# Input projection of a two-layer hybrid trunk: values projected last, pooling products inside the projection's last tiles

## The reference, cut to what matters

```
h      = rms_norm(x) * (1 + scale) + shift
proj   = h @ w_in                      # 1024 -> 1280 columns
q,k,v,u = split(proj, [512, 640, 768]) # 8 query heads, 2 key/value heads of 64; u: 4 groups of 128
q,k    = rms_norm per head; rotary positions on latent tokens; cached context keys and values joined
attn   = softmax(q k^T / 8) v          # in blocks of 128 queries
pooled = window mean(u) - u            # windows 2, 4, 8, 16, one per group
mixed  = pooled @ w_pool[group] * pool_scale
x      = x + gate * (concat(attn, mixed) @ w_out)
x      = x + gate * (silu(a) * g) @ w_down   # a, g: conv over rms_norm(x) @ w_up
```

## Time and profile before

| what | us |
|---|---|
| median of 3 runs | 1485.87 (1483.33 to 1486.97) |
| profiled execution, its own time | 1485.4 |
| its span | 1483.6 |
| TensorE busy | 1436.1 (97%) |
| VectorE busy | 896.4 (60%) |
| ScalarE busy | 518.3 (35%) |
| GpSimd busy | 388.3 (26%) |

### The profile page before, as it was taken

One profiled execution on the slowest core, in us unless ns is written; L12 is line 12 of the kernel. 1 busy time (PEld: TensorE's weight loads), 2 busy tenths in 40 slices (PEclk: granted clock), 3 DMA queues, 4 the chain that ended last, 5 costly groups with the idle time before them and its releaser, 6 DMA issues.

```text
span 1483.6 us, 25242 instructions
## 1 busy us (share of the span) xinstructions
PE 1436.1 (97%) x10077; PEld 1382.2 (93%) x10077; DVE 896.4 (60%) x1372; ACT 518.3 (35%) x743; POOL 388.3 (26%) x259
## 2 busy tenths in 40 slices
PE   6998899999999999999999989999999999999996
PEld 4888689999999999999999868999999999999996
DVE  3637867898875578784865788249844323444423
ACT  3325772442331123222242577234223112322321
POOL 0145001134431023443214600213433101333310
PEclk9999999999999999999999999999999999999998
DMA  9642004344444334334413200123322222222321
GB/s 340 211 172 74 1 2 129 99 128 129 141 143 127 127 105 150 124 113 138 138 40 86 61 2 1 54 90 103 114 80 82 79 68 72 71 71 80 89 59 71
DMA packets 190718, 147.05 MB, mean 99 GB/s; under 512 B 4256, under 2 KB 178984, under 8 KB 188584
## 3 DMA queue, kind: packets, MB, share of 16 engines
q1 hardware_dynamic: 189440, 145.32, 31.3%
q10 hardware_dynamic: 1192, 0.52, 0.1%
HBM read 142.94 MB, written 2.88 MB: 98 GB/s over the span
## 4 chain that ended last, share of the span: by engine, by line
PE 89%; DVE 5%; issue 2%; ACT 2%; DMA 1%; POOL 0%; SPq 0%; DVEq 0%; ACTq 0%; POOLq 0%
PE pair L1175 71%; PE pair L1192 5%; PE pair L1440 3%; PE pair L1476 3%; PE pair L1453 2%; DVE mod_acc L860 1%; PE pair L1262 1%; DVE w_lo L837 1%; DVE q_st L1006 1%; DMA xin<-in_x_sample_dram 1%; PE pair L1293 1%; PE pair L1245 1%; DVE conv L1119 0%; DVE x L932 0%; DMA mod_acc<-in_w_mod_dram 0%
## 5 line engine op out<-in xcount | busy, mean ns | idle before, releaser
L1175 PE MATMUL pair<-in_hi,w_hi 128*128 128x320 f32 x1792 | 410.5, 310 | 3.3 <-DVE w_lo L837 3.3
L1175 PE MATMUL pair<-in_hi,w_lo 128*128 128x320 f32 x1792 | 408.3, 309 | 0.0
L1175 PE MATMUL pair<-in_lo,w_hi 128*128 128x320 f32 x1792 | 408.3, 309 | 0.0
L1175 PEld LDWEIGHTS pair<-in_hi,w_hi 128*128 128x128 f32 x1792 | 298.9, 188 | 8.9 <-issue 4.3
L1175 PEld LDWEIGHTS pair<-in_hi,w_lo 128*128 128x128 f32 x1792 | 299.6, 188 | 0.0
L1175 PEld LDWEIGHTS pair<-in_lo,w_hi 128*128 128x128 f32 x1792 | 299.5, 188 | 0.0
L1119 DVE SCALAR_TENSOR_TENSOR conv<-pair,vec,conv 128x127 f32<-128x127 f32 x352 | 168.7, 541 | 200.1 <-ACT conv L775 199.9
L529 POOL TENSOR_TENSOR silu_a<-silu_a,conv 128x640 f32<-128x640 f32 x44 | 110.9, 2520 | 562.8 <-DVE conv L1119 562.8
L837 DVE TENSOR_TENSOR w_lo<-w_raw,w_hi 128x1024 fp32r<-128x1024 f32 (+1 forms) x152 | 201.7, 1327 | 62.4 <-ACT w_hi L550 62.1
L550 ACT ACTIVATE w_hi<-w_raw 128x1024 fp32r<-128x1024 f32 (+1 forms) x88 | 103.3, 1174 | 353.9 <-PE pair L1175 322.7
L775 ACT ACTIVATE conv<-pair,vec 128x640 f32<-128x640 f32 x88 | 77.8, 886 | 413.7 <-PE pair L1175 405.8
(11 more groups left out here) (171 smaller groups left out, 1544.9 us busy)
## 6 DMA issues: line engine op xcount, KB each, us to landing
w_raw<-in_w_up_dram SPq DMA_DIRECT2D x88, 512.0 KB, 3.9
mod_raw<-in_w_mod_dram SPq DMA_DIRECT2D x64, 512.0 KB, 4.4
w_raw<-in_w_down_dram SPq DMA_DIRECT2D x32, 704.0 KB, 4.6
w_raw<-in_w_in_dram SPq DMA_DIRECT2D x20, 512.0 KB, 4.0
w_first<-in_w_mod_dram SPq DMA_DIRECT2D x8, 1024.0 KB, 13.8
w_raw<-in_w_out_dram SPq DMA_DIRECT2D x16, 512.0 KB, 4.2
mod_raw<-in_w_mod_dram SPq DMA_DIRECT2D x4, 1024.0 KB, 6.7
mod_acc<-in_w_mod_dram SPq DMA_DIRECT2D x4, 1024.0 KB, 6.4
```

The lines of the kernel that those rows point to most:

```text
L1175: ins = pe.matmul(dst[:, a:a + HALF_T], w[:, s, k, :], rhs[:, kk, a:a + HALF_T], start=first and r == 0, stop=last and r == 2)
```

## The change

Ten tiles stay ten tiles, but the values come last: n = 5 to 8 are the queries and n = 9 the values.

- Key factors are made as columns like those of the queries (`rk`, 10 columns), inside the tile behind the keys, at k = 2. ScalarE's root and VectorE's reciprocal work on 10 columns. At k = 6 ten products of 64 result partitions with the identity (`k_factors`) spread them to a 128 x 640 PSUM area, which VectorE's scaling of the keys reads.
- The pooling product of a group (`mix_product`, two products instead of three) stands at k = 2 of tiles 6, 7, 8 and 9, the statistics of a query tile at k = 5. ScalarE copies a mixed group, scaled, to `u` (`mix_copy`). GpSimd parts the four groups into `in_hi` and `in_lo`, after its rotary work and after the projection's end.
- `keep_busy(15)` is gone.
- The values are transposed behind `scores(1)` and copied by ScalarE behind exponential 0.
- `q_hi(3)`, `q_low(3)` stand in unit 1, `q_hi(NQ)`, `q_low(NQ)` in unit 3 (they stood ahead of attention and in unit 2). The parting of the second output tile's weights (`hi` and `lo` of tile N_IN + 1) moves from the projection's last tile to unit 4. The two output transfers of new keys and values are issued in unit 6.
- The exponential's table is loaded by a `preload_act_table` ahead of attention. `k_low` is parted in two, one head group each, so scores of the first four heads wait for the first only.

```diff
-    IN_U, IN_K, IN_V, IN_Q = 0, NPOOL, NPOOL + 1, NPOOL + 2
-    IN_COLUMN = [AW + 2 * KV + P * g for g in range(NPOOL)] + [AW, AW + KV] + [P * t for t in range(NQ)]
+
+    IN_U, IN_K, IN_Q, IN_V = 0, NPOOL, NPOOL + 1, NPOOL + 1 + NQ
+    IN_COLUMN = [AW + 2 * KV + P * g for g in range(NPOOL)] + [AW] + [P * t for t in range(NQ)] + [AW + KV]
...
+                pool.wait_ge(s_lin, tile_in(L) + N_IN)
+                for g in range(NPOOL):
+                    pool.wait_ge(s_pc, L * NPOOL + g + 1)
+                    pool.tensor_copy(in_hi[:, NQ + g, :], u[:, g, 0:T]).then_inc(s_phi, 1)
+                    pool.wait_ge(s_phi, L * NPOOL + g + 1)
+                    pool.tensor_tensor(in_lo[:, NQ + g, :], u[:, g, 0:T], in_hi[:, NQ + g, :].bitcast(F32),
+                                       ALU.subtract).then_inc(s_plo, 1)
...
+                def mix_copy(g):
+
+                    act_e.wait_ge(s_pm, L * NPOOL + g + 1)
+                    act_e.activation(u[:, g, 0:TP], mix_p, ACT.Copy, scale=v(L, V_PS, g))
+                    act_e.activation(u[:, g, TP:T], mix_s, ACT.Copy, scale=v(L, V_PS, g)).then_inc(s_pc, 1)
...
+                    if n == IN_K:
+                        act_e.wait_ge(s_pkt, L + 1)
+                        act_e.activation(keys[:, TP:TP + PAST], pair[2][:, T:T + P], ACT.Copy).then_inc(s_pk, 1)
                         k_std()
...
+                        act_e.preload_act_table(ACT.Exp)
...
-                        if i == 2:
+                        if i == 3:
                             q_hi(NQ)
...
+                    if i == 0:
+                        values()
+                    if i == 1:
+                        q_hi(3)
+                    if i == 4:
+                        hi(tile_in(L) + N_IN + 1, (N_IN + 1) % 2, NK)
+                    if i == 6:
+                        new_cache_out()
...
+                    if i == 1:
+                        q_low(3)
+                    if i == 3:
                         q_low(NQ)
+                    if i == 4:
+                        lo(tile_in(L) + N_IN + 1, (N_IN + 1) % 2, NK)
...
-                    for hf in range(2):
-                        a = hf * HALF_T
-                        ins = pe.matmul(lin[2][:, a:a + HALF_T], head_ones, sq[:, E % 2, a:a + HALF_T], start=True, stop=True)
+                    for b in range(NT):
+                        c = K_STAT + 2 * b
+                        ins = pe.matmul(pair[3][:, c:c + 2], sq[:, E % 2, b * P:(b + 1) * P], head_ones[:, 0:P:HD],
+                                        start=True, stop=True)
                 else:
...
+            def k_factors(L):
+
+                pe.wait_ge(s_krs, L + 1)
+                pe.wait_ge(s_pk, L + 1)
+                for b in range(NT):
+                    for g in range(2):
+                        ins = pe.matmul(k_spread[g * HALF:(g + 1) * HALF, b * P:(b + 1) * P],
+                                        rk[:, 2 * b + g:2 * b + g + 1].to_broadcast([P, HALF]), ident, start=True, stop=True)
+                ins.then_inc(s_ksp, 1)
+
+            def mix_product(L, g):
+                if g == 0:
+                    pe.wait_ge(s_wp, 16 * (L + 1))
+                    pe.wait_ge(s_kn, L + 1)
+                else:
+                    pe.wait_ge(s_pc, L * NPOOL + g)
+                pe.wait_ge(s_pooled, L * NPOOL + g + 1)
+                pe.matmul(mix_p, wp[:, g, :], u[:, g, U_P:U_P + TP], start=True, stop=True)
+                pe.matmul(mix_s, wp[:, g, :], u[:, g, U_S:U_S + TS], start=True, stop=True).then_inc(s_pm, 1)
...
+                    def between(k, n=n):
+
+                        if n == IN_K + 1 and k == 2 or n > IN_K + 1 and k == 5:
+                            q_stat(L * NE + e_of(n - 1))
+                        if n == IN_K + 1 and k == 6:
+                            k_factors(L)
+                        if n > IN_Q and k == 2:
+                            mix_product(L, n - IN_Q - 1)
+                    linear(tile_in(L) + n, n % 2, NK, in_hi, in_lo, wait_k=between)
...
-                keep_busy(15)
-                for g in range(NPOOL):
-                    pe.wait_ge(s_pooled, L * NPOOL + g + 1)
-                    if g < 2:
...
+                def transpose_values():
+                    pe.wait_ge(s_free, L * (N_IN - NPOOL) + IN_V - IN_K + 1)
+                    pe.wait_ge(s_kout, L + 1)
+                    pe.wait_ge(s_pc, (L + 1) * NPOOL)
+                    for b in range(NT):
+                        ins = pe.transpose(pair[2][:, b * P:(b + 1) * P], v_feat[:, b * P:(b + 1) * P], ident)
+                    ins.then_inc(s_vt, 1)
...
                 scores(1)
+                transpose_values()
```

More of the change, by code:

```diff
@@ L220, in build @@
         MODP = 832
+        mix_s, mix_p = pair[2][:, 0:TS], pair[3][:, P:P + TP]
+        k_spread = pair[2][:, 0:T]
+        K_STAT = NQ * NT * 2
         V_BMOD, V_CONVB, V_N1, V_N2, V_PS, V_QG, V_KG = (0, 0), (0, 48), (0, 92), (0, 100), (0, 108), (0, 112), (0, 113)
@@ L1033, in _ @@
                         dve.tensor_copy(u[:, n, U_S:U_S + TS], src[:, TP:T]).then_inc(s_u, 1)
-                    lo(N + 2, n % 2, NK)
-                    if e_of(n - 1) is not None:
-                        if e_of(n - 1) == 0:
-                            k_norm()
-                        shuffle(e_of(n - 1))
+                    if n < N_IN - 1:
+                        lo(N + 2, n % 2, NK)
                     if 2 <= n < 2 + NPOOL:
                         window_end(n - 2)
+                    if n == IN_K:
+                        k_recip()
+                        k_norm()
+                        shuffle(0)
                     if n == IN_Q + 1:
-                        for g in range(KV // HD):
-                            for i, a in enumerate((g * HALF, (1 - g) * HALF)):
-                                dve.wait_ge(s_ks_hi, (L * 2 + g) * 2 + 1)
-                                own = slice(g * HALF, (g + 1) * HALF)
-                                dve.tensor_tensor(k_lo[a:a + HALF, g, :], keys[own, :], k_hi[own, g, :].bitcast(F32),
-                                                  ALU.subtract).then_inc(s_ks, 1)
-                    if n in (IN_Q + 2, IN_Q + 3):
-                        q_low(n - IN_Q - 1)
-                    if L == 0 and n == N_IN - 1:
-                        mod_finish(2)
-                        mod_finish(3)
-                for g in range(NPOOL):
-                    pool_low(g)
-                    if g == 0:
+                        shuffle(1)
+                        k_low(0)
+                    if n == IN_Q + 2:
+                        shuffle(2)
+                        q_low(1)
+                        k_low(1)
+                    if n == IN_Q + 3:
+                        shuffle(3)
+                        q_low(2)
+                        q_recip()
+                        if L == 0:
+                            mod_finish(2)
+                            mod_finish(3)
                         shuffle(NQ)
-                    if g == 1:
-                        q_recip()
-                q_low(3)
                 for i in range(NU + 1):
```

116 lines of the change are left out of this document (51 added, 65 removed).

## The result

The changed kernel takes 1494.2 us (median of 6 runs, 1491.97 to 1497.71), the kernel before 1484.66 in the same rounds: ratio 1.0066, 95% interval 1.0050 to 1.0082. It is 9.5 us slower; 1487.1 was forecast, within 1481.5 to 1493.0. The profiled execution has a time of 1494.2 and a span of 1492.4, against 1485.4 and 1483.6.

A forecast was written before the change was run, and what follows sets the result against it. TensorE's own list bounds the kernel, except in the change-over to attention, where a chain through other engines does. Projection +7.2, then a lead of 8.0 against 8.6 spent: +0.6 us a layer, 1487.1 us, range 1481.5 to 1493.

The forecast's parts named there:

- exponential 0 to 2: First attention units: values copy and query tile now stand between these exponentials; 7.1 us against 3.55, a loss of 3.55.
- 2 to 3: Between these exponentials, ScalarE alone sets the pace: 3.1 us against 3.29, a gain of 0.2.
- 3 to 4: Between these exponentials, VectorE's query subtraction begins 0.7 before the first: 3.0 us against 1.59, a loss of 1.4.
- 4 to 5: Between these exponentials, VectorE waits for ScalarE's weight half: 5.0 us against 1.59, loses 3.4, plus 0.6 for stretched `lo`.
- 5 to 6: Between these exponentials, VectorE's turn sets the pace: 1.59 us against 2.05, a gain of 0.45.
- 6 to 16: Unit 6 issues two transfers on ScalarE ahead of exponential 7: 0.3 us taken, between nothing and 0.8.
- Part 1: End of the input projection: work moved into tiles and new `k_factors` make the last tile end 7.2 us later.
- Part 2: Start of attention: first scores follow the last tile at once, exponential 0 at 845.3 instead of 853.33, a lead of 8.0.
- that rival: Projection tiles: statistics wait for ScalarE's copy, 1 us in three tiles a layer; +6, 1493 us; chance 0.05.
- part 3: First attention units: work formerly done before attention now stands between exponentials and spends the lead; sum -8.6 us.
- The second rival: First units: GpSimd locks out VectorE's scalings, TensorE at half clock into unit 7; +3 a layer, 1493 us; chance 0.20.
- The first rival: Attention: GpSimd does not stretch VectorE; -2.3 us a layer, 1481.3 us; chance 0.22.

The follow-up runs named there:

- run 5: Changed kernel with GpSimd's parting of the four pooling groups held back to exponentials 18, 24, 28 and 32, one each; 1486.6 us, ratio 1.0018.
- run 3: Changed kernel with 18, 4 and 8 products without use ahead of the scores of units 4, 6 and 7; 1491.9 us, ratio 1.0053.
- run 2: Changed kernel with both halves of the second output tile's weight parting moved from unit 4 to unit 12; 1494.0 us, ratio 1.0061.
- run 6: Changed kernel with both halves of the second output tile's weight parting moved from unit 4 to unit 21; 1493.3 us, ratio 1.0058.
- run 9: As run 5, with only VectorE's half of the second output tile's weight parting moved from unit 4 to unit 5; 1482.8 us, ratio 0.9983.
- run 11: As run 9, with 18 products without use ahead of the scores of unit 4; 1482.1 us, ratio 0.9985.
- run 1: Changed kernel with GpSimd's parting of the four pooling groups held back until exponential 12; 1493.9 us, ratio 1.0067.
- run 4: Changed kernel with the moves of run 1 and run 2 together; 1493.9 us, ratio 1.0060.
- run 12: Kernel before the change, without its 15 products without use (`keep_busy`) behind the last projection tile; 1485.4 us, ratio 1.0001.
- run 7: Changed kernel with the moves of run 5 and run 6 together; 1491.2 us, ratio 1.0035.

## Why the prediction was wrong

Second layer, us against before; each row is a term of the prediction's sum.

| term | forecast | measured |
|---|---|---|
| last tile ends later (46.75 from the key tile's end, 39.21 before) | +7.2 | +7.54 |
| tile's end to exponential 0 | -15.2 | -15.10 |
| exponential 0 to 2 | +3.55 | +4.89 |
| 2 to 3 | -0.2 | -0.31 |
| 3 to 4 | +1.4 | +2.71 |
| 4 to 5 | +4.0 | +3.14 |
| 5 to 6 | -0.45 | -0.46 |
| 6 to 16 (transfers, clock) | +0.3 | +2.51 |
| 16 to 39 | 0 | +0.04 |
| sum | +0.6 | +4.96 |

In the first layer exponential 39 comes 4.6 later than before, counted from the start of the execution. The two together, some 9.5, are near the 8.8 between the profiled executions. Half of the error lies ahead of exponential 6, which came 2.4 later instead of 0.3; the other half behind it, where the prediction had TensorE always supplied.

**What held.** Part 1: no wait inside a tile, `k_factors` 1.31 (1.5 taken, 2.3 feared). Part 2: exponential 0 came 2.0 behind the tile. The insertions did not stall the tiles, so that rival is out. The lead was there, 7.6 instead of 8.0, and was spent where part 3 said.

**What failed first: VectorE's small product and scalings at their lone durations, in the terms 0 to 2 and 3 to 4.** I stretched the query subtractions (2.66; measured 3.12 and 2.90) and, by half, `lo`, and nothing else. In 0 to 2, "maximum to exponential 1.05" took 2.32 (856.51 to 858.83), because the product took 1.44 instead of 0.16; that and the subtraction (+0.46) make about the error of 1.3, less 0.3 by which `q_low(3)` began earlier than I had it (an exponential with its read took 0.87, not 1.0). In 3 to 4 the 1.05 held (865.06 to 866.11). What failed there is "`q_low(NQ)` begins 0.7 before exponential 3": one product (+0.51) and two scalings (+0.33 each) stand ahead of it on VectorE, and it began 0.43 after. Run 5 took GpSimd's parting away: `q_low(NQ)` began 0.73 before exponential 3, and the two terms took 5.72 and 1.90. The Trainium skill, SBUF — State Buffer, "Who interferes with whom", has this: a VectorE instruction with two SBUF inputs contends with a GpSimd instruction that reads SBUF, and one with a single input only in a two-port mode. By that rule the product of two 128x1 columns counts as one with two inputs, whatever its size, and the maximum from PSUM does not count; the trace agrees (1.44 beside 0.81, as alone). The scalings, with a single input, were held up too: 0.88, 0.88 and 1.58 after and 1.85 in run 5 instead of 0.55, each with its end 0.34 or 0.35 behind that of the GpSimd instruction beside it. I had weighed the rule for the scalings and not looked for every instruction with two inputs on the chain.

**What failed second: the term 6 to 16, 0.3.** It held the price of two transfers and nothing for TensorE's clock. The transfers were sized rightly: they are issued in 0.34 and 0.45 us, and in run 3, which has them too, 6 to 7 takes 1.83, with 0.23 of idle time ahead of exponential 7. What cost nearly all of the 2.51 was TensorE at half its clock behind its wait of 2.77 for exponential 5 (run 3 gave back 2.8). The second rival named the clock and priced it at 2; I gave that rival 0.20, and with +3 a layer it would have been 1493. The measured 1494.2 lies close to its point, in part by luck: its other mechanism, scalings that wait for a whole GpSimd instruction, at 2 to 3 a layer, came to 0.66 on the chain, and the products, which cost 1.79, it did not have.

**4 to 5** was right in mechanism and 0.9 too dear: `lo` was not stretched (1.22), since GpSimd had ended. Its price was the wait, not the work: runs 2 and 6 moved the work and kept the price, and run 9 kept the work and took 4 to 6 from 7.14 to 5.53, where two undisturbed units take 3.18.

**The first rival** (no stretch, 1481.3) had the mechanism wrong, since GpSimd did stretch VectorE. Its price for a chain without stretch is nearly borne out: from exponential 0 to 16 run 5 takes 5.4 more than before, and that rival's sum has 5.7. Run 5 as a whole is not faster than before (1.0018), but it pays 1.9 and 2.2 for the parting in later units; without these it would be near 1482.6, an estimate from 1486.63 that no run tests. Run 9, with the weights' halves in two units, is faster (0.9983). What the 7 us of low clock a layer that remain in run 9 cost was tried in one way only, by the products of run 11, and stays open beyond that.

## What to carry to other kernels

Moving work off the engine that is the bound into a change-over is worth only what the chain there can take. Read that chain's smallest instructions too: here a product of 128x1 with two SBUF inputs lasted until the GpSimd instruction beside it had ended, however little it had to do. Then ask of each stretched instruction whether it is on the chain: the scaling that took 1.58 instead of 0.55 cost nothing. When work is moved between two engines that hand over, place the halves so that the second never waits with the chain's next step behind it; here that order was worth 3.9 us in the median, 2.2 of it found in the traces, and moving both halves together to another unit 0.9 at most. And when a move changes no time, look for where the gain was lost before dropping the theory: runs 1, 2 and 4 won 3.5 to 7 us a layer up to exponential 7 and had lost most of it again by the end of attention.

## What was not expected of the hardware

A 128x1 product on VectorE took 1.44, 1.37 and 1.32 us beside a GpSimd subtraction and ended within 0.02 us of it; alone it takes 0.16. TensorE's clock was at 0.50 to 0.52 for 6 to 9.5 us behind waits of 2.7 to 5.6 us. What that cost was nothing to be seen in run 9's exponentials 2 to 4 and in run 12's time, and 2.8 us a layer in exponentials 6 to 16 after and in 4 to 6 of run 7, by whether TensorE or the others set the pace there.
